# The last two expert turns of a two-layer decoder step: turn 7's gather and turn 5's rows go ahead of turn 6's products, and turn 7's gate and up products come in three parts

## What is computed

```python
def hier_moe(h, w_rg, w_re, w_gate, w_up, w_down):
    ...
    gates = jnp.sum(jax.nn.one_hot(expert_idx, N_EXPERTS, dtype=jnp.float32) * weights[..., None], axis=-2)
    hg = jnp.einsum('nld,edf->nlef', h, w_gate)
    hu = jnp.einsum('nld,edf->nlef', h, w_up)
    act = jax.nn.silu(hg) * hu * gates.astype(h.dtype)[..., None]
    return jnp.einsum('nlef,efd->nld', act, w_down)
```

## Time and profile before

| what | value |
|---|---|
| median of 3 runs | 1067.61 us (1065.2 to 1067.74) |
| the profiled execution | 1066.95 us |
| its span, first to last instruction | 1065.4 us |
| TensorE busy | 958.1 us, 90% of the span |
| VectorE, ScalarE busy | 424.8 us, 237.2 us |
| chain that ended last, by engine | PE 70%, DMA 19%, DVE 6%, ACT 2% |
| the DMA part of it | the up matrices of the experts, 19% |
| bytes read from HBM | 286.17 MB |

### The profile page before, as it was taken

One profiled execution on the slowest core, in us unless ns is written; L12 is line 12 of the kernel. 1 busy time (PEld: TensorE's weight loads), 2 busy tenths in 40 slices (PEclk: granted clock), 3 DMA queues, 4 the chain that ended last, 5 costly groups with the idle time before them and its releaser, 6 DMA issues.

```text
span 1065.4 us, 18014 instructions
## 1 busy us (share of the span) xinstructions
PE 958.1 (90%) x6766; PEld 572.6 (54%) x6766; DVE 424.8 (40%) x1107; ACT 237.2 (22%) x513; POOL 88.9 (8%) x199
## 2 busy tenths in 40 slices
PE   8999989899989999977769899999999999777695
PEld 7777767586884475533434344444444755234341
DVE  3733455465744356332434300252002553324343
ACT  3321136354201141101011311331002411000112
POOL 6333241140000000000000000000000000000000
PEclk9999999999979999988999999999999999989898
DMA  9951178795602689999999954443335899999994
GB/s 288 251 175 34 41 250 256 274 336 220 222 1 88 196 363 421 421 421 420 420 418 418 351 201 158 158 158 122 126 119 194 357 422 420 420 420 422 416 415 172
DMA packets 90063, 292.62 MB, mean 275 GB/s; under 512 B 16100, under 2 KB 52508, under 8 KB 62031
## 3 DMA queue, kind: packets, MB, share of 16 engines
q1 hardware_dynamic: 75508, 267.63, 65.4%
q0 software_dynamic: 5152, 17.05, 5.0%
q10 hardware_dynamic: 9306, 6.67, 2.0%
HBM read 286.17 MB, written 5.16 MB: 273 GB/s over the span
## 4 chain that ended last, share of the span: by engine, by line
PE 70%; DMA 19%; DVE 6%; ACT 2%; issue 1%; SPq 1%; ACTq 0%; DVEq 0%
DMA arena<-in_moe_w_up 19%; PE ps L1618 10%; PE ps L892 10%; PE ps L1372 9%; PE ps L1708 5%; PE ps L1358 3%; PE ps L1006 3%; PE ps L816 2%; PE ps L1019 2%; PE ps L807 2%; PE ps L1389 1%; PE ps L836 1%; PE ps L1611 1%; PE ps L1423 1%; PE ps L1095 1%
## 5 line engine op out<-in xcount | busy, mean ns | idle before, releaser
L1372 PE MATMUL ps<-arena,hT 128*32 128x512 f32 x896 | 112.9, 662 | 50.4 <-DMA arena<-in_moe_w_up 50.3
L1618 PE MATMUL ps<-arena,hT 128*128 128x512 f32 x256 | 111.0, 593 | 0.0
L892 PE MATMUL ps<-hT,arena 128*128 128x288 f32 x448 | 110.0, 407 | 0.0
L1358 PE MATMUL ps<-lvl,htok 128*128 128x128 f32 (+1 forms) x768 | 95.5, 281 | 7.9 <-DVE x L2610 7.7
L1372 PEld LDWEIGHTS ps<-arena,hT 128*32 128x32 f32 x896 | 33.9, 121 | 124.5 <-issue 124.5
L1358 PEld LDWEIGHTS ps<-lvl,htok 128*128 128x128 f32 x768 | 90.2, 191 | 15.8 <-issue 10.5
L892 PEld LDWEIGHTS ps<-hT,arena 128*128 128x128 f32 x448 | 84.6, 190 | 23.5 <-issue 0.5
L1618 PEld LDWEIGHTS ps<-arena,hT 128*128 128x128 f32 x256 | 48.3, 190 | 59.7 <-issue 59.4
L1475 PE MATMUL ps<-arena 128*128 128x512 f32 x112 | 55.3, 618 | 4.4 <-DVE x L2604 4.4
L1423 PE MATMUL ps<-arena 128*32 128x512 f32 x448 | 51.0, 595 | 0.0
L2596 DVE TENSOR_SCALAR hT<-ps,nw 128x128 f32<-128x128 f32 (+1 forms) x64 | 22.7, 355 | 68.5 <-PE ps L1358 68.4
(11 more groups left out here) (491 smaller groups left out, 1276.9 us busy)
## 6 DMA issues: line engine op xcount, KB each, us to landing
arena<-in_moe_w_gate SPq DMA_DIRECT2D x64, 1024.0 KB, 19.9
arena<-in_moe_w_up SPq DMA_DIRECT2D x64, 1024.0 KB, 21.4
arena<-in_moe_w_down SPq DMA_DIRECT2D x56, 1024.0 KB, 21.4
arena<-in_cache_k SPq DMA_DIRECT2D x64, 256.0 KB, 4.0
arena<-in_cache_v POOLq DMA_DIRECT2D x64, 256.0 KB, 4.0
arena<-in_w_in_odd SPq DMA_DIRECT2D x16, 1024.0 KB, 9.9
arena<-in_w_in_even SPq DMA_DIRECT2D x14, 1024.0 KB, 9.0
arena<-in_moe_w_down SPq DMA_DIRECT2D x16, 512.0 KB, 15.1
```

Source lines behind the costliest of these rows:

```text
L892: last = mm(ps[:, c % 4, 0:T], w[:, k, P * (c % 2):P * (c % 2 + 1)], hT[:, k, :], start=k == 0, stop=k == KD - 1)
L1358: last = mm(ps[:, row_bank(k), 0:w], htok[:, i, P * k:P * (k + 1)], pl[:, i, 0:w], start=i == 0, stop=i == 2)
L1372: last = mm(ps[EC * j:EC * (j + 1), q % 2, :], xgT[q % 2][:, k, EC * j:EC * (j + 1)], ring[:, sl:sl + 2, DE * k:DE * (k + 1)], start=k == ...
L1618: last = mm(ps[:, bank, :], hT[:, k, P * i:P * (i + 1)], ring[:, oslot(2 * n):oslot(2 * n) + 2, QC * k:QC * (k + 1)], start=k == 0, stop=k ...
```

## The change

It has three parts, in both layers.

**Loads of turn 7.** The four gate matrices come first, as whole units. The four up matrices follow as eight transfers of 512 KB: the first halves (k = 0 to 3) of all four, counted on the slot, then the second halves (k = 4 to 7), counted on a new semaphore `wu_half`. The down halves follow as before. A half of an up matrix is 4 KB in each partition, where a whole one is 8 KB and a half of a down matrix 2 x 2 KB.

**Products of turn 7.** `gate_part` takes all gates when they are there, then up over k = 0 to 3, then up over k = 4 to 7 behind `wu_half`.

**Order of turn 6.** The gather of turn 7 and the rows of turn 5 move ahead of turn 6's gate and up products; the places of turn 7 are made at the end of turn 5. The gather now waits for `xgd`/`xga` of turn 6 (the banks are free once its rows are copied), and the rows of turn 5 wait for those of turn 7.

A semaphore of the router (`rt_oh`) is merged into another (`rt_e4x`); nothing else moves there.

```diff
-        APART = (0,)
+        APART = (0, NQ - 1)
...
+            def up_half(layer, u, which, hf):
+                sl, cs = moe_slot(0, u), slice(UNIT // 2 * hf, UNIT // 2 * (hf + 1))
+                sp.dma_start(ring[:, sl, cs], WU[layer, bass.ds(which, 1)].rearrange("e (p k) f -> p (e k f)", p=P)[:, cs])\
+                    .then_inc(s.wu_half if hf else s_w[sl], 16)
...
                     first_free(layer, u)
-                    if u < MOE_UNITS - QE:
+                    if u < MOE_UNITS - 2 * QE:
                         moe_load(layer, 0, u, which)
+                    elif u < MOE_UNITS - QE:
+                        up_half(layer, u, which, 0)
                     else:
+                        if u == MOE_UNITS - QE:
+                            for v in range(MOE_UNITS - 2 * QE, MOE_UNITS - QE):
+                                up_half(layer, v, sp.value_load(perm[0:1, place_of(v):place_of(v) + 1], min_val=0,
+                                                                max_val=NE - 1), 1)
                         down_half(layer, u, which, 0)
...
                                 W(s.p_rdy, NQ, q + 1)
-                                if q >= 2:
+                                if q == NQ - 1:
+                                    rows_taken(q - 1)
+                                elif q >= 2:
                                     W(s.xadd, 5 * NQ, 5 * (q - 1))
...
+                        elif q == NQ - 1 and part == 1:
+                            pe.wait_ge(s.wu_half, 16 * QE * (layer + 1))
...
                         W(s.pw_rdy, NQ, q + 1)
-                        if q:
+                        if q == NQ - 3:
+                            W(s.xgd, 4 * NQ, 4 * NQ)
+                        elif q:
                             W(s.xadd, 5 * NQ, 5 * q)
...
+                            if q == NQ - 3 and j == 1:
+                                W(s.xga, 4 * NQ, 4 * NQ)
...
                         if q:
-                            if q == NQ - 1:
+                            if q == NQ - 2:
+                                gather(q + 1, range(KD))
+                            if q >= NQ - 2:
                                 out_rows(q - 1)
-                            gate_up(q, range(KD))
+                            if first and q == NQ - 1:
+                                gate_part(q, range(KD), 0)
+                                gate_part(q, range(KD // 2), 1)
+                                gate_part(q, range(KD // 2, KD), 1)
+                            else:
+                                gate_up(q, range(KD))
...
-                            if q < NQ - 1:
+                            if q < NQ - 2:
                                 out_rows(q - 1)
                             act_turn(q)
-                            if q + 1 < NQ:
+                            if q < NQ - 2:
                                 gather(q + 1, range(KD))
```

More of the change, by code:

```diff
@@ L1327, in moe @@
                 spin(0, 14)
-                pe.wait_ge(s.rt_oh, layer + 1)
+                pe.wait_ge(s.rt_e4x, 3 * layer + 2)
                 mm(rk[:, 0:2, :], ut, ohs[:, 0:2, :], start=False, stop=False, skip_group_check=True)
@@ L1963, in moe @@
                 scale_rows(n_, 2)
-                act.wait_ge(s.rt_e4x, 2 * layer + 1)
+                act.wait_ge(s.rt_e4x, 3 * layer + 1)
                 A_(e4, d4, ACT.Exp).then_inc(s.rt_exp2, 1)
@@ L1967, in moe @@
                     scale_rows(n_, i)
-                act.wait_ge(s.rt_e4x, 2 * layer + 2)
+                act.wait_ge(s.rt_e4x, 3 * layer + 3)
                 A_(ex2, ex2, ACT.Exp).then_inc(s.rt_exp2, 1)
@@ L2490, in moe @@
                 V.tensor_tensor(d4, lg[:, :, 0:NG], bc(m4, [P, 3, NG]), ALU.subtract).then_inc(s.rt_e4x, 1)
-                dve.wait_ge(s.rt_e4x, 2 * layer + 1)
+                dve.wait_ge(s.rt_e4x, 3 * layer + 1)
                 ch(V.tensor_scalar(eq4, d4, 0.0, None, ALU.is_ge))
@@ L2509, in moe @@
                 first_of(oh2, eqa, NE, 0)
-                V.tensor_tensor(ohs, oh1, oh2, ALU.add).then_inc(s.rt_oh, 1)
+                V.tensor_tensor(ohs, oh1, oh2, ALU.add).then_inc(s.rt_e4x, 1)
                 V.tensor_tensor(ex2, v2, v1, ALU.subtract).then_inc(s.rt_e4x, 1)
@@ L2657, in turn @@
                     def turn(q):
[L2658 removed]
+                        if q < NQ - 2:
                             places(q + 1)
+                        elif q == NQ - 2:
+                            rows_in(q + 1)
+                            rows_out(q - 1)
                         if first and q == 0:
@@ L2677, in turn @@
                                 .then_inc(s.hot_dve, 1)
-                        if q + 1 < NQ:
+                        if q < NQ - 2:
                             rows_in(q + 1)
+                        if q == NQ - 3:
+                            places(NQ - 1)
                         if first and q == NQ - 1:
```

11 lines of the change are left out of this document (6 added, 5 removed).

## The result

The changed kernel takes 1073.8 us, the kernel before 1067.3 us beside it: ratio 1.0067, with a 95% interval of 1.0053 to 1.0081. It is slower. The forecast of 1062.0 us and its range are missed on the other side. The profiled execution has a span of 1071.8 us where that of before has 1065.4.

What follows compares the result with a forecast made beforehand. Weight transfers bound the expert turns, then a TensorE, ScalarE and VectorE chain behind the last up matrix. 1066.95 - 3.0 - 2.5 = 1061.45 us for the profiled execution, 1062.0 on the median; range 1058.5 to 1066.5.

Steps and rivals of the forecast that it cites:

- the move costs nothing: Turn 6: gather and rows fit the 7.55 us weight wait; products end 1.1 us later, gates still start at 1029.5.
- it does not run dry: Transfer queue at turn 7's up halves: over 10 us of work stays queued, SP passing turn 6's products about 1 us later.
- The case of a lost cover: Ahead of turn 7's gates: without the 7.55 us wait as cover, up to 5.3 us a layer return; no chance given.
- Slower: TensorE stays at 1.2 GHz through the whole end of both layers: Rival, end of turn 7: low clock costs 9 us a layer before slack and gain, giving 1075; chance 0.05.
- if the gates wait for something that I overlook: Turn 7's gates: an unseen wait, the order not holding, leaves 1067.6; within a rival of chance 0.09.
- the 0.09: Rival: gain lost elsewhere or change not doing what it says, 1065.1 or 1067.6; chance 0.09.
- Three parts: Turn 7's products: only 1.8 of 7.1 us stays behind the last up matrix; first down half could start 5.3 us earlier.
- The loads as the next bound: Turn 7's down halves: their landing sets the start, 0.4 us later for 4 KB pieces; gains 3.0 and 2.5 us.
- The rival with a fixed cost for each transfer: Rival, turn 7's loads: each added transfer holds the queue 1.4 us, giving 1073.3; chance 0.01.
- The old order is the obstacle for the parts: Turn 6: with the old order of gather and rows, turn 7's gates could start only at 1037.4, so the move is needed.
- The clock rival: Rival, turn 7: waits lower the clock, first down half 1.9 us slower; 1065.3 in both layers, 1063.7 in one; chance 0.27.
- Gain lost in the mixer's weights: After the first layer: its gain meets a wait for the next mixer's weights, leaving 1065.1; within chance 0.09.

Runs made afterwards that it cites:

- e2: Kernel before, with the branch on the overflow flag taken out of TensorE, ScalarE and VectorE: 1067.5 us, ratio 1.001.
- e10: Changed kernel with ten never-run matmuls added in TensorE's branch body, shifting the code behind it: 1064.2 us, ratio 0.998 against the kernel before.
- e1: Changed kernel without the branch ahead of turn 6 on TensorE, ScalarE and VectorE: 1065.1 us, ratio 0.998 against the kernel before.
- e6: Changed kernel with the branch moved two turns earlier, ahead of turn 4: 1063.1 us, ratio 0.9963 against the kernel before.
- e9: e6 with idle products in turn 7, six before the second up halves and four before the first down half: 1063.4 us, ratio 0.9972 against the kernel before.
- e4: Kernel before with the halves of up and the three-part product alone, in the old order: 1067.1 us, ratio 1.0009.
- e5: Changed kernel with the branch moved one turn earlier, ahead of turn 5: 1068.6 us, ratio 1.0016 against the kernel before.
- e8: Changed kernel loading only 512 of 2048 columns of each whole matrix from turn 5 on: 1052.3 us, single comparison without an interval.

## Why the prediction was wrong

**The step that failed** is "the move costs nothing", in the part on the moved gather and rows. The gather and the rows were added up without a term between the end of the down product and their start. It took TensorE's 7.55 us wait as free time, because the profile names a transfer as its releaser. The wait was free of work but not free: it covered the code fetch behind the branch, which ended first and so left no mark on TensorE. In the second layer of the changed kernel TensorE spent 3.50 + 4.60 us in the stalls and 3.0 us more on a gather at low clock, 11.1 us where the step had counted zero.

The prediction's step "it does not run dry" fell with it: it let SP pass turn 6's products about 1 us later, and it was 15 us, 3.8 of them brought along from the first layer.

The same part also had a price: "If this cover were gone, up to 5.3 us would come back onto the chain in each layer". 1062.0 + 2 x 5.3 = 1072.6 is near the measured 1073.8, but that is luck. The 5.3 us are what the three parts save on TensorE (7.1 - 1.8), and the forecast had counted only 3.0 and 2.5 of them as gained, since the loads come next. With the whole 5.3 back, the chain is that of the kernel before, 1067.6. To be 6 us slower than that it takes the stalls and the slow gather themselves, 11.1 us, less the slack. The case of a lost cover was named and given no chance of its own; what else used the cover was not asked.

**It was there to be read.** VectorE goes through the same branch and did not wait for weights. Its timeline in the kernel before, second layer, first work behind the branch:

```profile
1000.39 0.69 DVE L2683 COPY arena<-ps 128x512 f32<-128x512 f32 x1 [3.92 <-PE ps L1423]
1005.95 0.68 DVE L2574 TENSOR_SCALAR lvl<-code,arena 128x128 f32<-128x128 f32 x3 [4.88 <-issue]
```

4.88 us between two operations of one engine with nothing to wait for, at the place where the code has an `If`; in the first layer it is 5.0. The waits grouped by line have it in one row:

```profile
DVE lvl L2574 <- issue: 9.9, 2, 5.0
```

This is the fetch with its price, on another engine. That it belongs to the branch e2 shows: there the same operation follows the copy at once, in the second layer as below, and the row is gone.

```profile
1000.58 0.69 DVE L2665 COPY arena<-ps 128x512 f32<-128x512 f32 x1 [3.92 <-PE ps L1423]
1001.19 0.67 DVE L2556 TENSOR_SCALAR lvl<-code,arena 128x128 f32<-128x128 f32 x3
```

With it the gates of turn 7 would have been forecast up to 4.9 us later, at 1034.4, and the three parts without a wait to 1034.4 + 7.1 = 1041.5, silu's copy 2.1 later at 1043.6: still just ahead of the left halves at 1044.3. So one stall of this size uses up the slack and hardly costs anything, which is what e10 shows (1064.2). Two stalls break the case, and the second one is in no row of the kernel before: it depends on where the changed code comes to lie. The right reading would have been a rival of its own, no gain or a loss of some us, and its size could not have been read off.

**The rivals.** None had the fetch. "Slower: TensorE stays at 1.2 GHz through the whole end of both layers" (0.05) came near the time, 1075, by another mechanism: the clock was low for the gather, behind the stalls, not from the second half of up to the end. "if the gates wait for something that I overlook" (in the 0.09) was nearest to the cause and priced at 1067.6, no change, as if an overlooked wait could only take the gain away.

**What held**, seen once the stalls are out of the way (e1, e6, e9):

- *Three parts.* In the second layer the last quarter of the products takes 1.93 us in e1 (forecast 1.8) and 2.73 in e6, behind a wait of 3.10 and 2.98 us (3.3).
- *The loads as the next bound.* In e1 the last left and right halves of down land at 1031.0 + 12.4 = 1043.4 and 1038.1 + 10.5 = 1048.6 (forecast 1044.0 and 1049.2), and the first down half starts at 1043.76. The earlier trace rows has 1043.6 and 1048.8, and e1's second layer starts 0.5 us earlier than that of before, so the pieces of 4 KB cost at most 0.3 us where 0.4 was taken (by turn 5, whose products start at 976.97 in both, nothing is left of the 0.5). The rival with a fixed cost for each transfer is out.
- *The old order is the obstacle for the parts.* e4 has no gain.
- *The clock rival* (0.27) is right as a mechanism, and it was undersized: it counted 1.9 us for the slow down half; in the second layer the second half starts 9.1 and 9.0 us behind the first in e1 and e6 instead of 5.1, so 3.9, because the rows between are slow too (1.07 + 3.78 us in e1 instead of 0.63 + 1.98). In the first layer it is 6.4 and 6.8, so 1.3 and 1.7, as counted.
- *Gain lost in the mixer's weights* (part of the 0.09) is real in e9, 1.3 us.

With the branch two turns earlier the change gives a ratio of 0.9963. On the median that the forecast started from, 1067.6, this is 1063.7 us: the number of the clock rival in one layer, 1.7 over the forecast's own. That the two numbers meet is chance, since e6's profile has the low clock in both layers. The sum came near for what it summed, and missed one term that stood in no row of the engine it looked at.

**What stays open.** Why e5 is 5.5 us slower than e6 in the median while its profiled execution is the fastest of the two; its stalls in turn 5 are what shows as a difference, but in the second layer turn 5's products start at 976.93 behind one, as in the kernel before (976.97). Why the second stall is as long as 4.6 to 4.8 us, longer than the first. And what decides whether the clock falls: the dip in the mixer, and the down half, which in the second layer of e10 takes 3.37 us behind waits of 0.45 and 2.41 us and in that of e5 1.92 behind 1.18 and 2.37.

## What to carry to other kernels

An idle time that ends with a transfer says what came last, not that nothing else was going on in it. Before work is moved into such a wait, look for what else ends inside it, first of all a branch, and read its price from an engine that passes the same branch without the cover: an "issue" wait in its row. Put a branch where each engine has a long wait for data anyway. If a change of a few lines costs several microseconds at a place where no engine waits for another, shift the code or move the branch before giving up the change.

## What the runs showed of the hardware

- Behind a taken branch TensorE stood 3.4 to 3.7 us while the DMA engines were full of weights, and 1.2 us with them at 13% (e8, first layer). VectorE stood 4.9 to 5.0 us where it had work at once, 2.1 with light traffic, and not at all without the branch.
- A second stall of 4.6 to 4.8 us (2.9 with light traffic) a few matmuls on, in straight code, is there or not depending on ten never-run matmuls in front of it: 9.6 us of 1073.8.
- A stall of this kind also costs clock: the gather behind two of them took 8.6 us instead of 5.6, behind one 7.2.
- Waits of 3.10 and 2.42 us, with 1.93 us of products and the transposes between them, were followed by the lower clock for the down half (e1). With ten idle products in these waits the down halves ran at 1.92 us (e9).
